# Packing the levels of a gated linear attention stage, in a two-model kernel on one core

## The reference, cut to what matters

```python
def step(C, n, m):                      # mLSTM, one chunk
    s = einsum("bhtd,bhsd->bhts", qc, kc) * exp(d - mt)
    num = einsum("bhts,bhsv->bhtv", s, vc) + ...
    den = sum(s, axis=-1) + ...
    h = num / maximum(abs(den), exp(-mt))

def step(S):                            # GLA, one chunk; b is the running sum of log decays
    A = einsum("bhtd,bhsd,bhtsd->bhts", qc, kc, exp(b_t - b_s))   # t >= s only
    o = einsum("bhts,bhsv->bhtv", A, vc) + einsum("bhtd,bhdv->bhtv", qc * exp(b), S)
# forward and backward scans over context, then latent tokens; both directions are added
```

## Time and profile before

| | us |
|---|---|
| median of 3 runs | 3411.18 |
| lowest and highest run | 3410.55, 3412.18 |
| span of the profiled execution | 3409.5 |
| the mixing stage in it | 243.3 to 432.3, 189.0 long |

### The profile page before, as it was taken

One profiled execution on the slowest core, in us unless ns is written; L12 is line 12 of the kernel. 1 busy time (PEld: TensorE's weight loads), 2 busy tenths in 40 slices (PEclk: granted clock), 3 DMA queues, 4 the chain that ended last, 5 costly groups with the idle time before them and its releaser, 6 DMA issues. The chain is left out here.

```text
span 3409.5 us, 68412 instructions
## 1 busy us (share of the span) xinstructions
PE 3127.3 (92%) x27432; PEld 2612.1 (77%) x27432; DVE 2430.7 (71%) x3693; ACT 1834.7 (54%) x3101; POOL 478.4 (14%) x502
## 2 busy tenths in 40 slices
PE   6998889999989798879999999998999999999997
PEld 4774456887765577768988799766888988988896
DVE  5867575448574644567786688645799999999996
ACT  2533334223222665534443644755778888888875
POOL 0000003441100121105613211331000000000000
PEclk8999989999989999998998999998999999999998
DMA  6530033437141000036663497602799999999994
GB/s 223 170 93 1 1 120 122 148 105 247 62 133 41 2 5 4 5 111 214 213 247 106 156 379 293 179 26 69 284 365 355 377 356 362 377 357 363 367 359 185
DMA packets 287315, 646.20 MB, mean 190 GB/s; under 512 B 24477, under 2 KB 144393, under 8 KB 286921
## 3 DMA queue, kind: packets, MB, share of 16 engines
q1 hardware_dynamic: 266169, 566.81, 47.0%
q0 software_dynamic: 20160, 73.41, 5.9%
q10 hardware_dynamic: 720, 2.23, 0.2%
HBM read 641.34 MB, written 1.05 MB: 188 GB/s over the span
## 5 line engine op out<-in xcount | busy, mean ns | idle before, releaser
L4836 DVE TENSOR_TENSOR weights_lo<-raw_ring,weights_hi 128x896 fp32r<-128x896 f32 (+1 forms) x376 | 413.2, 1126 | 50.6 <-ACT weights_hi L4789 41.0
L4789 ACT ACTIVATE weights_hi<-raw_ring 128x896 fp32r<-128x896 f32 (+1 forms) x376 | 366.6, 985 | 90.3 <-PE bank_pair L4759 85.3
L4759 PE MATMUL bank_pair<-weights_hi,expert_x_hi 128*128 128x448 f32 x1024 | 294.3, 369 | 5.0 <-DVE weights_lo L4836 5.0
L4759 PE MATMUL bank_pair<-weights_hi,expert_x_lo 128*128 128x448 f32 x1024 | 291.8, 366 | 0.0
L4759 PE MATMUL bank_pair<-weights_lo,expert_x_hi 128*128 128x448 f32 x1024 | 291.8, 366 | 0.0
L4836 DVE TENSOR_TENSOR weights_lo<-H,weights_hi 128x896 fp32r<-128x896 f32 (+1 forms) x240 | 264.0, 1133 | 22.4 <-ACT weights_hi L4789 14.2
L4789 ACT ACTIVATE weights_hi<-H 128x896 fp32r<-128x896 f32 (+1 forms) x240 | 236.8, 990 | 68.5 <-PE bank_pair L4759 68.5
L2668 DVE SCALAR_TENSOR_TENSOR conv<-bank_pair,vec,conv 128x189 f32<-128x189 f32 (+3 forms) x396 | 138.6, 430 | 145.2 <-ACT conv L2628 145.2
L4759 PEld LDWEIGHTS bank_pair<-weights_hi,expert_x_hi 128*128 128x128 f32 x1024 | 189.8, 188 | 21.0 <-issue 4.8
L4759 PEld LDWEIGHTS bank_pair<-weights_hi,expert_x_lo 128*128 128x128 f32 x1024 | 192.8, 188 | 15.9
L4759 PEld LDWEIGHTS bank_pair<-weights_lo,expert_x_hi 128*128 128x128 f32 x1024 | 192.6, 188 | 16.0
(11 more groups left out here) (831 smaller groups left out, 8471.8 us busy)
## 6 DMA issues: line engine op xcount, KB each, us to landing
raw_ring<-in_moe_w_gate SPq DMA_DIRECT2D x72, 896.0 KB, 6.9
raw_ring<-in_moe_w_up SPq DMA_DIRECT2D x64, 896.0 KB, 7.3
ring_up<-in_ffn_w_up SPq DMA_DIRECT2D x110, 512.0 KB, 4.0
raw_ring<-in_moe_w_down SPq DMA_DIRECT2D x48, 1024.0 KB, 7.2
mod_ring_ada<-in_w_ada POOLq DMA_DIRECT2D x84, 512.0 KB, 6.5
H<-in_moe_w_up SPq DMA_DIRECT2D x48, 896.0 KB, 7.4
ring_down<-in_ffn_w_down SPq DMA_DIRECT2D x66, 512.0 KB, 6.5
H<-in_moe_w_down SPq DMA_DIRECT2D x32, 1024.0 KB, 7.3
```

The costliest lines, as they stand in the source:

```text
L4759: ins = nc.tensor.matmul(banks[half][:, 0:b - a], x, w[:, a:b], start=start and i == 0, stop=stop and i == 2)
L4789: nc.scalar.activation(hi[:, u % CUTS, 0:n].bitcast(F32R), raw_part(u), ACT.Copy).then_inc(cut.sem, 1)
L4836: nc.vector.tensor_tensor(lo[:, u % CUTS, 0:n].bitcast(F32R), raw_part(u)[:, 0:n], hi[:, u % CUTS, 0:n], ALU.subtract).then_inc(parted.sem, 1)
```

## The change, and its diff

1. `MixSteps.gla` is a list of 26 steps in place of 44: per direction two diagonals or none, seven levels, NEAR, FAR once for each channel pair, PV once for each. A level step now covers both channel pairs.
2. Only the late half of the tokens has queries in a level. `qs` and `eqk` hold the late and the early halves packed (512 columns for both channel pairs), so a level step has 16 matmuls of 64 columns in place of 8 of 128, and the bank pair is filled by both channel pairs. `copy_predicated` takes this packed bank into the late places of `att`, which now lies in `st.H`, 2048 columns for each direction.
3. The diagonal is made once for both directions, times two, into `att[0]`; `att[1]` is set to zero.
4. `shift` runs on GpSimd, for step i+3; one exp of 1024 columns replaces two of 256.
5. `add_keys` on GpSimd sums the four `pt` of a head, and `sum_keys` on PE multiplies the sum by the ones once (512 columns) in place of a matmul after each item.
6. `pt` has four slots; the items end at step 22 (`LAST`), `invert(1)` and the last `norm`s are put beside the last GLA steps; the forward numerators go to `st.Y`.

```diff
-    PER = LEVELS + 3
-    STEPS = 4 * PER
-    ITEMS = 8 * 4
+    NEAR, FAR, PV = LEVELS, LEVELS + 1, LEVELS + 2
+    ITEMS, LAST = 8 * 4, 22
...
+        levels = lambda d, a, b: [(d, l, None) for l in range(a, b)]
+        far = lambda d: [(d, self.FAR, c) for c in (0, 1)]
+        self.gla = [(0, 0, 0), (0, 0, 1)] + levels(0, 1, self.FAR) + far(0)
+        self.gla += levels(1, 1, 2) + [(0, self.PV, 0)] + levels(1, 2, 3) + [(0, self.PV, 1)]
+        self.gla += levels(1, 3, self.FAR) + far(1) + [(1, self.PV, 0), (1, self.PV, 1)]
+        self.STEPS = len(self.gla)
+        self.pairs = [i for i, (d, l, c) in enumerate(self.gla) if 0 < l < self.PV and c != 1]
...
+        def shift(eng, ns, i):
+
+            e = M.pair_no(i)
+            d, l, _ = M.gla[i]
+            bq, bk, ref = halves(ev.decay[:, d], l, d)
+            if e >= 2:
+                eng.wait_ge(scaled.sem, scaled.at(e - 1))
+            ns.tensor_tensor(packed(eqk[:, e % 2, 0], l), bq, ref, ALU.subtract)
+            ns.tensor_tensor(packed(eqk[:, e % 2, 1], l), ref, bk, ALU.subtract).then_inc(shifted.sem, 1)
+
+        def add_keys(eng, ns, m):
+
+            u, s, runs = M.items[m]
+            eng.wait_ge(pt_ready.sem, pt_ready.at(m + 1))
+            if m % 4 == 1:
+                eng.wait_ge(pt_used.sem, pt_used.at(m))
+            else:
+                eng.wait_ge(keys_added.sem, keys_added.at(3 * u + m % 4 - 1))
+            for a, b in runs:
+                total = pt[:, M.slot(4 * u), a * P:b * P]
+                ins = ns.tensor_tensor(total, total, pt[:, M.slot(m), a * P:b * P], ALU.add)
+            ins.then_inc(keys_added.sem, 1)
+
+        @block.gpsimd
+        def _(pool):
+            nc.gpsimd.memset(ks[:], 0.0).then_inc(zeroed.sem, 1)
+            for i in M.pairs[0:2]:
+                shift(pool, nc.gpsimd, i)
+            nc.gpsimd.memset(att[1], 0.0).then_inc(zeroed.sem, 1)
+            for i in range(M.STEPS):
+                if M.opens(i + 3) and i + 3 not in M.pairs[0:2]:
+                    shift(pool, nc.gpsimd, i + 3)
+                for m in M.items_of(i):
+                    if m and (m - 1) % 4:
+                        add_keys(pool, nc.gpsimd, m - 1)
+            add_keys(pool, nc.gpsimd, M.ITEMS - 1)
...
-                for r, (a, b) in enumerate(runs):
-                    x = pt[:, m % 2, a * P:b * P]
-                    flags = dict(start=j == 0 and r == 0, stop=j == 3, skip_group_check=True)
-                    nc.tensor.matmul(NUM[:, a * P:b * P], ev.v[:, 0, s, h * P:(h + 1) * P], x, **flags)
-                    ins = nc.tensor.matmul(DEN[32 * h:32 * h + 32, a * P:b * P], st.C("ones")[:, 0:32], x, **flags)
-                ins.then_inc(pt_used.sem, 1)
+            def sum_keys(u):
+                h = M.heads[u][1]
+                pe.wait_ge(keys_added.sem, keys_added.at(3 * u + 3))
+                if u == ML_HEADS:
+                    pe.wait_ge(den_copied.sem, den_copied.at(1))
+                nc.tensor.matmul(DEN[32 * h:32 * h + 32], st.C("ones")[:, 0:32], pt[:, M.slot(4 * u)], start=True, stop=True).then_inc(den_summed.sem, 1)
...
-                if l in INSIDE:
-                    tiles = [(b * P, b * P, b * P, P) for b in range(4)]
+                elif l < NEAR:
+                    tiles = [(64 * n, ks[:, e % 2, n * P:(n + 1) * P], qs[:, e % 2, 64 * n:64 * n + 64]) for n in range(8)]
...
-                nc.scalar.activation(x, x, ACT.Exp)
-                nc.scalar.activation(y, y, ACT.Exp).then_inc(exps.sem, 1)
+                nc.scalar.activation(eqk[:, e % 2], eqk[:, e % 2], ACT.Exp).then_inc(exps.sem, 1)
...
             for i in range(M.STEPS):
-                shift(i + 2)
-                scale(i + 1)
+                if M.opens(i + 1):
+                    scale(i + 1)
                 for m in M.items_of(i):
                     if m + 1 < M.ITEMS:
                         mask(m + 1)
+                    product(m)
...
+                if i == M.LAST + 1:
+                    invert(1)
                 add_up(i)
+                if i >= M.STEPS - 2:
+                    for h in (0, 1):
+                        norm(ML_HEADS + 2 * (i - M.STEPS + 2) + h)
```

More of the change, by code:

```diff
@@ L2148, in even_mix_stage @@
     M = MixSteps()
-    INSIDE, NEAR, FAR, PV = range(LEVELS), LEVELS, LEVELS + 1, LEVELS + 2
+    NEAR, FAR, PV = M.NEAR, M.FAR, M.PV
     with ExitStack() as ctx, core.engines_block() as block:
         sb = lambda name, shape: core.sb(name, shape, ctx=ctx)
-        masked, weight, pt = sb("masked", [P, 2, P]), sb("weight", [P, 2, TT]), sb("pt", [P, 2, TT])
+        masked, weight, pt = sb("masked", [P, 2, P]), sb("weight", [P, 2, TT]), sb("pt", [P, 4, TT])
         den, num, maxb, every = sb("den", [P, TT]), sb("num", [P, ML_HEADS, TT]), sb("maxb", [P, 2, TT]), sb("every", [4, P])
[L2154 to L2159, removed]
+        eqk, qs, ks = sb("eqk", [P, 2, 2, TT]), sb("qs", [P, 2, TT]), sb("ks", [P, 2, 2 * TT])
+        near, far = sb("near", [P, 2 * TT]), sb("far", [P, 2, 2, 2, CTX])
+        att = [st.H[:, 4 * d:4 * d + 4] for d in (0, 1)]
+        zeroed, shifted, exps, scaled, scored, summed, moved, out_copied, out_added = (
+            core.counter("gla_" + n) for n in ("zeroed", "shifted", "exps", "scaled", "scored", "summed", "moved", "out_copied", "out_added"))
+        spread, max_copied, scores, masked_ready, weights, pt_ready, pt_used, num_copied, keys_added, den_summed = (
+            core.counter("ml_" + n) for n in ("spread", "max_copied", "scores", "masked_ready", "weights", "pt_ready", "pt_used", "num_copied", "keys_added", "den_summed"))
         floor_ready, floored, den_copied, inverted, inv_ready, normed, every_ready = (
@@ L2169, in turn_bank, with late_first, halves @@
             return TURN[M.at[kind, i] % 2]
[L2171 to L2175, removed]
-            ref = v[:, :, early, 0:1] if d else v[:, :, early, h - 1:h]
-            return v[:, :, late], v[:, :, early], ref.to_broadcast([P, TT // (2 * h), h])
+        def late_first(l, d):
+            return d and l < FAR
+        def halves(x, l, d):
+            h = 1 << (l - 1)
+            v = x.rearrange("p c t -> p (c t)").rearrange("p (n two h) -> p n two h", two=2, h=h)
+            late, early = (0, 1) if late_first(l, d) else (1, 0)
+            ref = v[:, :, early, 0:1] if d else v[:, :, early, h - 1:h]
+            return v[:, :, late], v[:, :, early], ref.to_broadcast([P, TT // h, h])
@@ L2279, in _ @@
                         add_item(m - 1)
[L2280 to L2283 removed]
+                    if m >= 5 and m % 4 == 1:
+                        sum_keys(m // 4 - 1)
+                if i == M.LAST:
+                    add_item(M.ITEMS - 1)
+                    use_turn("floor", 1)
+                    sum_keys(len(M.heads) - 1)
+                if i >= M.STEPS - 2:
+                    for h in (0, 1):
+                        use_turn("inv", ML_HEADS + 2 * (i - M.STEPS + 2) + h)
         @block.scalar
```

247 lines of the change are left out of this document (118 added, 129 removed).

## The result

The changed kernel takes 3355.9 us (median of 4 runs, 3349.5 to 3360.1) against 3410.9 (3408.5 to 3412.2) before it: 0.983 of the time, 95% interval 0.981 to 0.986. Run again with more rounds it took 3352.0 against 3411.2, ratio 0.984 (0.982 to 0.985). The forecast was 3365 with a range of 3347 to 3385; the gain is 55 to 59 us where 46 were forecast.

A forecast was written before the change was run, and what follows sets the result against it. PE, not full and waiting mostly for DVE, was to bound the inner steps after the change; 19.3 less work, 18.1 less waits and 8.8 less rest make 46 us, so 3365 us, range 3347 to 3385.

The forecast's parts named there:

- PE's queue: PE's work in the mixing stage: 141.1 us before, 121.8 after, 19.3 less.
- Waits: PE's waits left around the mixing stage: 14.0 us against 32.1, 18.1 less.
- the loop above, 6: Part of PE's 14.0 us of waits: 6 us from the way round through GpSimd, ACT and DVE.
- the way round: Inner steps: scale, two shifts, exp, weights, products, copy, next scale; 9.4 us over two steps, 4.7 each, level with PE.
- rival 2: Inner steps: the way through GpSimd sets the pace, with shifts at 1.66 us and DVE's scales held; 3376 to 3395, 22%.
- The rest: Stage time beyond PE's work and waits, ends and slow clock: 15.8 us to 7, 8.8 less; choice 3 to 13.
- DVE: DVE's busy time in the stage falls by about 46 us to 82, with 1.1 us of slack per inner step.
- The end: Behind the stage's last PV stand its addition and two norms with their additions, some 4 us.
- 1: Mixing stage PE-bound with waits about halved, the forecast itself: 3355 to 3376 us, 55%.
- 3: Cheap loads and few waits: level step 1.6 us, waits 7, rest 3; 3340 to 3355 us, 15%.
- 4: GpSimd slower by far on low levels' short runs; at 5.5 us a shift the whole takes 3436 us; 5%.
- 5: Waits of PE only change their names: still 32 us, the rest stays 15.8; 3392 us, 3%.

The follow-up runs named there:

- shifts twice: The changed kernel with GpSimd computing each pair of decay shifts twice, the second over the first: 3384.0 us, again 3378.6.
- shifts on VectorE: The changed kernel with the 36 decay shifts moved back from GpSimd to VectorE: 3362.2 us, again 3361.9.
- the edits at the start and in the reciprocal: Against the changed kernel, separately: first pair of shifts ahead of the clearing of ks, 3358.3 us; forward reciprocal in four pieces, 3355.3 us.
- the three together: The changed kernel with first shift before clearing ks, forward reciprocal in pieces, and all backward norms between the backward PVs: 3358.6 us.
- the end behind: The changed kernel with backward maximum, reciprocal, spread rows and norms put back behind the last PV and its addition: 3360.5 us.
- the norms between: The changed kernel with all four backward spread rows and norms between the two backward PVs: 3352.1 us.
- the denominators by item: The changed kernel with denominators again one TensorE product per numerator piece and no key sums on GpSimd: 3365.5 us.
- the half columns: The changed kernel with level matmuls cut to 32 moving columns forwards and 64 weight columns backwards: 3354.5 us, one run.

## Why the prediction was right, step by step

**One sum holds for all of them.** A level step takes 2.00 at the full clock and 3.68 at the lower one (the changed kernel's first profile):

```profile
316.51 3.68 PE L2332 MATMUL bank_pair<-qs,ks 64*128 64x64 f32 x32
```

so a us at the lower clock loses 1 - 2.00 / 3.68 = 0.46. Take from each stage its waits and 0.46 of its low us. (What PE waits at the lower clock is then taken off one and a half times; in the two runs of shifts twice that makes the remainder 2 to 3 us too small.) The changed kernel leaves 121.9 and 121.3, shifts on VectorE 121.6 (twice), shifts twice 120.8 and 120.3, the edits at the start and in the reciprocal 121.4 and 121.7, the three together 121.5; the end behind 120.3 and the norms between 120.9, which also move rows at the end. Denominators by item leave 136.5. All but the denominators by item lie within 1.6 us. So the stage is PE's queue, its waits and its clock, and the forecast can be read term by term.

**PE's queue** was forecast at 141.1 before and 121.8 after. After it, 121.9 and 121.3 less the 2.5 us of norms behind PE's last row (377.9 to 380.37) are 119.4 and 118.8; before, 188.9 - 30.5 - 15.7 less 2.2 of such norms are 140.5. The level steps came out at 14 x 1.93 = 27.0 (27.4 forecast), with the chosen price of the earlier trace rows and its reason confirmed by the half columns; the bound from the earlier trace rows, 1.6, was wrong for weights of 128 columns. The rule of the Trainium skill that a load costs its columns and not its rows (TensorE: Matmul & The Clock Gate, LDWEIGHTS) agrees in kind for the columns (no run here varies the rows): 64 columns in place of 128 take 1.08 in place of 1.93; its 107 ns compare with 121 measured here (1.93 / 16). The denominators were forecast at 13.6 less; undone, the stage's remainder rises by 15.0. The queue's term was right within 1 to 3 us.

**Waits**: forecast 14.0, measured 8.7 and 6.6 by the same count (with the 1.6). This is the mis-sized term. Of its parts the start, the hold before the backward PV (1.2; 1.4 forecast) and the maximum (1.1; 3 forecast) are there; "the loop above, 6" is not. In the first profile PE waits for scaled keys once, at 254.1, and for products twice, at 251.7 and 258.6, all of it at the start. The forecast had put the way round level with PE's 4.7. PE's pace was right: in the first profile its second and its seventh forward level step start at 262.52 and 286.00, 4.70 a step. The way round was too dear, with shifts at 1.3 and exp at 1.2; they take 1.08 and 1.05 (ACT's group of 18, mean 1054), and its sum becomes 4.4. But the same sum is too cheap in another term: the two scales last 1.48 and not 1.2, which gives 4.5, and the other terms were not measured in their places. So it is shown that the loop cost nothing after the start; its slack, 0.2 to 0.3 a step, is an estimate. Doubled shifts brought waits of the size of rival 2's, but at a few places and in part by the key sums, not in each step.

**The rest**, 15.8 to 7 by the forecast: clock and end together. By the 0.46 the clock cost 15.7 before and 6.3 or 4.7 after, and 2.5 of end are left. The size is right; the reason given (half the waits, about half the slow stretches) is too simple. Four profiles with 4.4 to 5.5 of waits have 10.2 us at the lower clock, a fifth with 5.5 has 27.3. Within the changed kernel's family more waits mostly went with more time at the lower clock (3.8 with 3.7; 9.4 with 34.1, twice; 15.4 and 18.2 with 64.9 and 58.3), but before the change 30.5 went with 34.1. What makes one stretch 3.4 and another 17.1 us long stays open.

**DVE**: forecast 82, measured 95. The copies of levels 1 and 2 take twice the price of the earlier trace rows (4 x 1.2 = 5 more), a scale 0.78 in place of 0.6 (6 more), and the masks 0.47 in the mean, 0.34 without GpSimd's shifts. Spread over 14 steps that is 0.9, less than the forecast's slack of 1.1 a step, and PE does not wait for it. **POOL**: 61 in place of 64. **The end**: as forecast, 4.4 against "some 4".

**The rivals.** 1 is what happened in kind, TensorE bound and fewer waits, but the time is at its lower edge (3355) or under it: 3355.9, and 3352.0 again, which lies in the stretch of 3. 2 and 4 failed by the shift's price; 5 by the waits. 3 had the few waits right (7), the cheap loads wrong, and its rest of 3 too small (7 to 9). What the parts of the change are worth, undone one at a time against the second profile, in waits, work and clock together: the denominators and key sums 11.0, the shifts on GpSimd 15.7, the end 7.7. The packing, the scales and the diagonal were not undone alone.

## What to carry to other kernels

Price a step of small matmuls by its weight columns (shown here for 32 and 64 moving columns), and halve those, not the moving ones, if the step is to get cheaper. Where PE sets the pace, a short wait costs its length and what the clock loses behind it: in two kernels here the clock, by the 0.46, took 1.7 to 2.5 times what the added waits did (why is open), while work put back on PE cost less than its length. Before a stretch of a single profile is explained, look whether a kernel that differs only later in time has it. And when a sum for a loop through several engines comes level with the pace, read from the trace where the waits stand: the sum gave their size here and not their places.

## What the runs showed of the hardware

A memset of GpSimd holds even a small copy of DVE. POOL and DVE in order of time at the start of the changed kernel's stage:

```profile
245.09 1.80 POOL L2231 MEMSET ks<- 128x2048 f32 x1 [180.18 <-POOLq L206]
245.12 1.85 DVE L2510 COPY every<-const 4x128 f32<-4x128 f32 x1 [0.30 <-PEq L206]
...
246.86 1.04 POOL L2213 TENSOR_TENSOR eqk<-decay 128x512 f32<-128x512 f32 x1
...
246.89 2.20 DVE L2471 SCALAR_TENSOR_TENSOR masked<-maxb,const 128x128 f32<-128x128 f32 x2
```

The copy of 4x128 lasts from 0.03 behind the memset's start to 0.08 behind its end, and two masks of 0.29 each last 2.20 beside two shifts. With the shift first, the copy starts together with it and is done in 0.21:

```profile
243.99 1.12 POOL L2213 TENSOR_TENSOR eqk<-decay 128x512 f32<-128x512 f32 x1 [178.93 <-SPq L206]
243.99 0.21 DVE L2510 COPY every<-const 4x128 f32<-4x128 f32 x1 [0.30 <-PEq L206]
```

Here the shift takes 1.12 in place of 1.04, which fits a short hold of GpSimd, though single shifts elsewhere vary as much. The Trainium skill (SBUF — State Buffer, SBUF: two separate sides) gives the shared ports to whoever starts first, for the whole instruction; the held copy, 1.85 in place of 0.21, agrees. A fp32 copy from SBUF to SBUF counts there among the instructions that take both pairs of ports. DVE is busy 94.9 us with the memset first and 91.9 with the shift first, and of these 3 us PE's waits show 0.6 at most (5.0 against 4.4).

GpSimd subtracts and adds at an even price, 1.08 for 512 columns in the mean (single ones up to 1.28), 0.53 for 128 in the key sums, whatever the length of the runs. A masked copy of DVE with elements in runs of one or two costs 2.44 for 1024 columns, in longer runs 1.23 to 1.32. And one and the same kernel had stages of 131.0 and 135.3 in two profiles: by the 0.46, 1.6 of the 4.3 us are the lower clock, which the forecast treated as a remainder, and 2.1 are waits of PE.
